# Issuing the first conditioning weight loads from SP without two waits, in a three-layer diffusion-style block

## The reference, cut to what matters

```
mod   = silu(c)     @ w_ada[0] + b_ada[0]
mod_c = silu(c_ctx) @ w_ada[0] + b_ada[0]
sh1, sc1, ... = split(mod, 6)           # likewise for mod_c
h  = rms_norm(x,   norm_mix[0]) * (1 + sc1)  + sh1
hc = rms_norm(ctx, norm_mix[0]) * (1 + sc1c) + sh1c
b_gate, c_gate, u = split(h @ conv_w_in, 3)   # the first large product
```

## Time and profile before

| what | us |
|---|---|
| median of 3 runs (lowest to highest) | 2005.49 (2004.65 to 2007.55) |
| the profiled execution, its own time | 2006.4 |
| its span in the profile | 2004.7 |
| PE busy in the span | 1939.6 |
| DVE busy | 826.2 |
| ACT busy | 282.5 |
| POOL busy | 305.6 |

### The profile page before, as it was taken

How to read it: one execution, slowest core, us unless ns; L and a number is a source line. 1 busy time by engine, 2 the same in 40 slices (tenths; PEclk the granted TensorE clock), 3 DMA queues, 4 the chain that set the end, 5 groups by cost and what they waited for, 6 DMA issues and landing times.

```text
span 2004.7 us, 25452 instructions
## 1 busy us (share of the span) xinstructions
PE 1939.6 (97%) x10672; PEld 1307.2 (65%) x10672; DVE 826.2 (41%) x1353; ACT 282.5 (14%) x603; POOL 305.6 (15%) x267
## 2 busy tenths in 40 slices
PE   6999999999999999999999999999998999999998
PEld 2444458888888874457888888768785555445444
DVE  2556437888885355273434213575224100000001
ACT  2000020000000121163000011251202100000000
POOL 0000115555543250000111011300000000000000
PEclk8999999999999999999999999999998999999999
DMA  9554204444541270003976451230027999999997
GB/s 404 196 172 161 91 22 147 167 157 160 177 171 73 88 312 0 0 1 133 407 257 231 168 213 66 111 143 28 4 103 303 408 429 429 429 429 429 429 428 311
DMA packets 48782, 420.22 MB, mean 210 GB/s; under 512 B 5441, under 2 KB 5457, under 8 KB 22961
## 3 DMA queue, kind: packets, MB, share of 16 engines
q1 hardware_dynamic: 29376, 344.73, 42.2%
q0 software_dynamic: 18880, 71.18, 10.6%
q10 hardware_dynamic: 432, 2.96, 0.4%
HBM read 417.81 MB, written 1.05 MB: 209 GB/s over the span
## 4 chain that ended last, share of the span: by engine, by line
PE 81%; DMA 8%; DVE 6%; issue 3%; ACT 2%; SPq 0%; DVEq 0%; ACTq 0%
PE PS L1281 8%; PE PS L1411 8%; PE PS L1046 8%; PE PS L1013 8%; PE PS L1056 6%; DMA ring<-w_moe 6%; PE PS L1123 6%; PE PS L1470 4%; PE PS L1432 4%; PE PS L1269 4%; PE PS L1108 4%; DVE SC L1813 3%; PE PS L1143 3%; PE PS L1445 3%; PE PS L1239 2%
## 5 line engine op out<-in xcount | busy, mean ns | idle before, releaser
L1281 PE MATMUL PS<-ring,A 128*64 128x512 f32 x1024 | 223.6, 593 | 4.0 <-DMA ring<-w_moe 3.2
L1281 PEld LDWEIGHTS PS<-ring,A 128*64 128x64 f32 x1024 | 73.9, 137 | 150.4 <-issue 141.4
L1813 DVE SCALAR_TENSOR_TENSOR SC<-A,CS,SC 128x512 f32<-128x512 f32 x208 | 164.8, 845 | 10.1 <-DMA A<-ada 8.2
L1411 PE MATMUL PS<-A,ring 128*128 128x512 f32 x368 | 159.7, 594 | 0.0
L1046 PE MATMUL PS<-A,ring 128*128 128x256 f32 x704 | 156.2, 383 | 1.2 <-ACT A L598 1.2
L1013 PE MATMUL PS<-ring 128*128 128x256 f32 x672 | 150.9, 380 | 0.0
L1046 PEld LDWEIGHTS PS<-A,ring 128*128 128x128 f32 x704 | 134.1, 192 | 23.3 <-issue 5.2
L1013 PEld LDWEIGHTS PS<-ring 128*128 128x128 f32 x672 | 126.9, 190 | 24.6 <-issue 7.7
L1411 PEld LDWEIGHTS PS<-A,ring 128*128 128x128 f32 x368 | 69.4, 190 | 89.8 <-issue 89.8
L449 POOL DMA_DIRECT2D ring<-ada x64 | 34.5, 539 | 539.7 <-DVE SC L1813 347.5
L1269 PE MATMUL PS<-ring,A 128*64 128x512 f32 x512 | 113.4, 595 | 0.7 <-ACT A L700 0.7
(11 more groups left out here) (366 smaller groups left out, 2499.5 us busy)
## 6 DMA issues: line engine op xcount, KB each, us to landing
ring<-w_moe SPq DMA_DIRECT2D x96, 2048.0 KB, 18.7
ring<-w_fin SPq DMA_DIRECT2D x44, 1024.0 KB, 7.2
ring<-ada POOLq DMA_DIRECT2D x64, 512.0 KB, 4.5
A<-ada POOLq DMA_DIRECT2D x64, 512.0 KB, 4.5
ring<-w_fout SPq DMA_DIRECT2D x16, 1408.0 KB, 6.8
ring<-w_conv SPq DMA_DIRECT2D x8, 1536.0 KB, 14.8
ring<-w_qkv SPq DMA_DIRECT2D x6, 2048.0 KB, 16.0
ring<-w_win SPq DMA_DIRECT2D x6, 2048.0 KB, 10.4
```

The source lines that it names most:

```text
L1281: mm = pe.matmul(PS[CAP * e:CAP * (e + 1), g, :], XG[:, k * P + e * CAP:k * P + (e + 1) * CAP], slot("moe", k // 2, w, w + 512), start=(k ...
L1411: mm = pe.matmul(PS[:, 3 * (j % 2) + c, :], slot("conv", j, k * 384 + c * 128, k * 384 + c * 128 + 128), h_of(k, 512), start=(k == 0), sto ...
L1813: ins = dve.scalar_tensor_tensor(out=ACC[:, i, :], in0=w, scalar=scale, in1=ACC[:, i, :], op0=ALU.mult, op1=ALU.add)
```

## The change

The two waits at the head of SP's program are taken away, and nothing is put in their place.

```
--- before.py
+++ after.py
@@ -380,8 +380,6 @@
                 sp.dma_start(ring[:, o:o + size], W[stage][n]).then_inc(
                     sem(f"landed{s + LANDED.get(stage, 0)}"), 16)
 
-            sp.wait_ge(sem("vecs_in"), 16)
-            sp.wait_ge(sem("consts_in"), 16)
             sig = {name: k for name, _, _, _, k in STREAM}
 
             def consumed(name, i):
```

## The result

The changed kernel takes 2013.2 us in the median of 7 runs (2011.2 to 2013.71), against 2005.49 before (2004.65 to 2009.45 over 7 runs). The ratio is 1.0025, with a 95% interval from 1.0015 to 1.0035: a small loss, about 5 us. Repeated later beside another set of runs of before, it is 1.0026 (1.0015 to 1.0036). The medians of the first runs lie 7.7 us apart, outside that interval of 3 to 7 us, and those of the repeat 5.2; the text goes by the ratio. The forecast was a loss of 2.1 us; the sign held, the size was less than half of what came. The median of 2013.2 by itself lies above the stated range; the ratio, put on 2005.5, gives 2010.5, inside its upper edge of 2010.9.

What follows compares the result with a forecast made beforehand. The prediction took PE to bound the kernel, except in the first 50 us; PE's `ada0` products ending at 38.8 instead of 36.73 gave 2.1 us on the median 2005.5: 2007.6 us, range 2003.4 to 2010.9.

Steps and rivals of the forecast that it cites:

- The wait of 5.0 us is not worth 5.0 us: SP's start: DMA engines are already busy, so the earlier issue wins 0.5 us there and slot 3 comes 0.7 us earlier.
- X late, by turns of rows: ACT's loads: engines alternate rows of the two queues, so X lands at 23.5 us with slot 2; chance 0.50.
- the 1.2 us taken off X: X's landing: full turns gave 24.7 us; 1.2 was subtracted because X before came at 11.9 against a reckoned 13.1.
- The products behind X: PE after X: squares, the norm's last short products and 48 products of slots 1 to 3, ending at 38.8 us.
- Rival C: PE's slower clock falls into the 48 products, 1.6 us more, and X in full turns, 1.2: loss 4.9, 2010.4; chance 0.11.
- V, C and PE's start cost nothing: PE's start moves from 15.7 to 16.9 us behind later V and C; costed at nothing, since X is later still.
- The start of the sum: PE's end of slot 3 at 36.73 us before, against which 38.8 after gave the 2.1 us loss.
- Carried one to one: From PE's end of the `ada0` products to the kernel's end: the whole shift of 2.1 us reaches the end.
- Rival A: DMA engines take whole loads in turn: X lands at 19.9 us, a gain of 1.6, 2003.9 us; chance 0.17.
- Rival B: ACT's loads keep most of their rate, sharing by bytes: X at 16.9, 2004.8 us; chance 0.20 including nothing.
- The bounds on X: X's landing: between 16.9 us (sharing by bytes) and 24.7 us (turns in full).

Runs made afterwards that it cites:

- The kernel with X first: Changed kernel with ACT's three loads issued in the order X, V, C; ratio to before 1.0052 (1.0040 to 1.0065).
- the short rows: Changed kernel with each `ada0` load cut into four of 1024 columns, so its rows are 4 KB; ratio to before 1.0000 (0.9988 to 1.0011).
- the queue: Changed kernel with V, C and X issued by SP ahead of `ada0`, all in one queue; ratio to before 0.9996 (0.9987 to 1.0005).
- the kernel before with PE's order changed: Kernel before, waits kept, with PE's short norm products moved behind `ada0` slots 0 to 2; ratio to before 1.0001 (0.9991 to 1.0012).
- The kernel with PE's order changed: Changed kernel with PE's short norm products moved behind `ada0` slots 0 to 2; ratio to before 0.9999 (0.9990 to 1.0008).

## Why the prediction was right or wrong

**The wait of 5.0 us is not worth 5.0 us.** Right. The engines were the limit, and slot 3 came 0.9 us earlier where 0.7 were reckoned. The reasoning for it was wrong, and that is luck: no bytes were won up to 6 us (1.43 MB moved, not 1.72), since the engines again began slowly, at 180 and 363 GB/s. The kernel with X first, whose rows are all long, began no faster (186 and 317 GB/s), so the short rows are not shown to be the reason; it stayed open. By the stretches the 11.35 MB were moved by about 29.1 us in both kernels; what shrank is slot 3's landing behind them, from 2.3 us to 1.4.

**X late, by turns of rows.** Right in kind, and the packets of the two queues and the experiments on the rows, the order and the queue show it. V was forecast at 8.9 and came at 9.8, C at 15.0 and came at 15.9, X at 23.5 and came at 25.7.

**The step that failed first: the 1.2 us taken off X.** In full turns the sum was 24.7. I took 1.2 off because X before had come that much sooner than turns would give, if `ada0` shared with it from 7.1 us on. It did not. The kernel before, from 5.8 to 9 us and from 9.4 to 9.6, where SP's first packets stand (columns as above):

```profile
q10 hardware_dynamic: 82, 1.34, 100.1%
```
```profile
q10 hardware_dynamic: 3, 0.05, 57.3%
q1 hardware_dynamic: 2, 0.03, 38.2%
```

`ada0`, issued at 5.86, moved its first row only at about 9.5, 3.7 us behind the issue, when X had some four of its 128 rows left. In the changed kernel, where it met idle engines, that took about 1.0 us, and the forecast assumed 1.15 for both. So before, X had hardly shared at all. With nothing beside it, in the kernel that waits for X, X landed at 12.0, no sooner than the 11.9 of before: its landing has a tail of its own that the average rate doesn't show (DMA share 0.43 and 0.08 in its last stretches above; after 10.0 us two rows of its 128 were left). The comparison from which the correction came didn't measure the turns. How little one landing says is seen in the kernel before with PE's order changed: by the same loads X came at 13.1, where `ada0` again moved nothing before 8.5. Without the correction the forecast would have been 3.3 us of loss. The rest of X's lateness, 1.0 us, is about that by which V and C were late; the 0.29 MB not moved by 6 us are 0.7 of it.

**The products behind X.** From X's landing to the copy 15.9 us passed, where 15.3 were reckoned. The last of the norm's products ended 0.7 us behind the squares instead of 0.35, and the 48 products took 10.84 instead of 10.56. In the kernel with X first, at the full clock, the same 48 took 10.47. The granted clock of the changed kernel in these microseconds:

```profile
28.00:29.00 1.00, 0.92 (x16) 0.36 (x16) 0.00 (x0) 1.00 (x3) 0.00 (x0) 0.64 1.09 463
29.00:30.00 1.00, 1.00 (x22) 0.40 (x16) 0.00 (x0) 1.00 (x3) 0.00 (x0) 0.50 0.93 393
...
31.00:32.00 1.00, 1.00 (x6) 0.15 (x4) 0.21 (x1) 0.75 (x2) 1.00 (x3) 0.65 0.99 418
```

The granted clock fell to 0.50 at about 28.3, after PE's idle time and a stretch of sparse work, and was back before 32. Rival C put such a fall behind the squares and priced it at 1.6 us; it happened, for the most part under their cover, and cost about 0.6. C named both terms that were off, X in full turns and the clock, and its total of 4.9 is close to what came; but it had them at 1.2 and 1.6, and they were 2.2 and 0.6, so the nearness of the total is an accident.

**V, C and PE's start cost nothing.** Right: PE started at 18.05 instead of the 16.9 reckoned and was done with slot 0 at 23.3; X was later still. The kernel with PE's order changed shows the same late start without a loss.

**The start of the sum.** The 36.73 us of before, from which the 2.1 were reckoned, hold the last slot's products at the lower clock, 5.3 us. None of the seven other kernels that work this slot on its own shows that again (3.60 us each). The saving of this clock, which the forecast took as a property of the kernel, was one of the profiled execution.

**Carried one to one.** Right within what can be told, though the figures agree better than they ought to: +4.89 at the copy, +3.70 at PE's first convolution product (46.71 against 43.01, since before had the lower clock in the short products between), +5.00 at `cout` (since PE's first 32 convolution products then took 9.84 us instead of 8.54), +5.7 at the end of the profiled span, and 3 to 7 by the interval of the ratio. The steps at the first convolution product and at `cout` are clock levels at which the two profiled executions differ.

**Rival A, whole loads in turn**, with ACT's queue served first, would have had V in at 3.9, C at 10 and X at 19.9. V was at 9.8. With SP's queue served first (an order that the forecast left out) V, C and X would have been as late as by rows, but one of X and slot 0 would have been in at 8.1 in the kernel with X first, and neither was before 13.6. By the Trainium skill, "DMA: Bandwidth & Descriptors", section "Queues, rings and completion order", an engine drains a packet of typically 9 to 17 descriptors before it turns to another queue; with eight rows of each load per engine (128 rows on 16 engines) that would have been a whole load. What the landings and the packet counts show here is a finer turn, and turns of one row give all landings to within some 1.5 us. **Rival B**, sharing by bytes, is excluded by the short rows, by X first (V at 19.6 instead of 14.5) and by the bytes of the two queues above (1.79 MB to 0.31).

**The chances.** 0.12 for a loss over 0.2% was low for what came, 0.25%. The bounds on X, 16.9 to 24.7, did not hold it at 25.7 either: they were taken from the reckoning and not widened for the lag of a landing, which slot 3 had already shown to reach 2.3 us.

## What to carry to other kernels

A load that is issued earlier on a second queue takes its engine time from what the first queue is loading, and a load of short rows loses most beside one of long rows, because the two are served row by row. How much it takes depends on what has begun: here `ada0` halved the turns of ACT's loads when both queues began together, and got nothing for 3.7 us when it was issued onto engines that already had X. Before a wait ahead of a large load is removed, look whether the small things behind which the work starts are in, and what the consumer's written order puts behind the load that will now be last. Small loads that are wanted first belong ahead of the large ones in the same queue, or the large ones start when they are nearly in.

## What the runs showed of the hardware

- Two queues shared the engines by rows: V, 0.34 MB in rows of 2.6 KB, took 3.0 us alone, 5.5 beside rows of 4 KB and 8.9 beside rows of 16 KB.
- While both queues had work, they moved about equally many rows: 123 and 126 packets from 4 to 9 us, with 1.79 and 0.31 MB.
- A load that was issued while another queue's load kept the engines busy moved its first row 3.7 us later (issued at 5.86, first packet at 9.5, and at 3.83 and 7.5 in the kernel that waits for V alone); onto idle engines it took about 1.0 us.
- X took 10.2 us from issue to landing with no other load beside it and 10.1 with `ada0` moving from 9.5 us on, though its bytes at 430 GB/s would have been moved by about 9 us.
- PE's clock level at the last `ada0` slot and at the norms differs between executions: 16 products took 5.3 us in one and 3.6 in another, and 32 products at the attention norm 7.1 or 10.0 us. This alone moves a time by some microseconds and can explain part of the 2003 to 2015 us over which runs of before scatter. Which executions get which level stayed open.
